# Two layer norms in each of two layers, rebuilt: squares relative to a mean of half the stream, the last two slabs tile by tile, no loop over layers

## The reference

```
for l in range(2):
    proj = x @ w_in                        # pool, q, k, v, conv and gate columns
    merged = sum of three gated branches   # pooling, windowed attention, short convolution
    x = layer_norm(ALPHA * x + merged @ w_o, ln1_g, ln1_b)
    up = causal_dwconv(x @ w_up, ffn_conv_w)      # 3 taps, D_FF_2 = 2816
    a, b = split(up, 2)
    x = layer_norm(ALPHA * x + (silu(a) * b) @ w_down, ln2_g, ln2_b)

def layer_norm(x, g, b):
    mu  = mean(x);  var = mean(square(x - mu))
    return (x - mu) * rsqrt(var + 1e-5) * g + b
```

## Time and profile before

| what | us |
| --- | --- |
| median of 3 runs | 3015.32 (3015.03 to 3015.91) |
| profiled execution | 3016.21 |
| its span, first to last instruction | 3014.4 |
| PE busy | 2943.7 (98%) |
| ACT busy | 1600.8 (53%) |
| DVE busy | 1022.2 (34%) |
| POOL busy | 411.4 (14%) |

### The profile page before, as it was taken

How to read it: one execution, slowest core, us unless ns; L and a number is a source line. 1 busy time by engine, 2 the same in 40 slices (tenths; PEclk the granted TensorE clock), 3 DMA queues, 4 the chain that set the end, 5 groups by cost and what they waited for, 6 DMA issues and landing times.

```text
span 3014.4 us, 36389 instructions
## 1 busy us (share of the span) xinstructions
PE 2943.7 (98%) x13318; PEld 2389.8 (79%) x13318; DVE 1022.2 (34%) x2094; ACT 1600.8 (53%) x2309; POOL 411.4 (14%) x477
## 2 busy tenths in 40 slices
PE   8999999999999999999998999999999899999997
PEld 6889888888886678888887887888877788788885
DVE  4533535321214754112135114323242511432324
ACT  6655656544445755444556445545454644454544
POOL 1111111111111001111110111111111011111111
PEclk9999999999999999999999999999999999999999
DMA  8666767788886319888882896787867398688785
GB/s 236 148 150 134 163 134 154 152 196 192 192 194 149 84 41 203 193 195 192 193 194 64 198 194 136 190 199 179 201 151 173 78 193 192 135 196 183 194 195 140
DMA packets 138147, 503.52 MB, mean 167 GB/s; under 512 B 15472, under 2 KB 15728, under 8 KB 137872
## 3 DMA queue, kind: packets, MB, share of 16 engines
q0 software_dynamic: 68016, 248.22, 46.6%
q1 hardware_dynamic: 69120, 251.69, 27.2%
q10 hardware_dynamic: 864, 1.65, 0.2%
HBM read 499.40 MB, written 2.10 MB: 166 GB/s over the span
## 4 chain that ended last, share of the span: by engine, by line
PE 87%; DVE 4%; DMA 3%; ACT 3%; issue 2%; DVEq 1%; ACTq 0%
PE ps L937 72%; PE ps L955 5%; DMA wl<-weights 3%; PE ps L1040 1%; PE ps L979 1%; PE ps L1097 1%; PE ps L1260 1%; ACT wl L418 1%; PE ps L1242 1%; PE ps L1241 1%; DVE arena L1906 1%; DVEq L1910 1%; DVE arena L1972 1%; PE ps L1314 0%; PE ps L1080 0%
## 5 line engine op out<-in xcount | busy, mean ns | idle before, releaser
L417 ACT ACTIVATE wh<-raw 128x1024 fp32r<-128x1024 f32 (+1 forms) x470 | 495.1, 1053 | 1103.4 <-PE ps L937 1055.6
L937 PE MATMUL ps<-HH,wh 128*128 128x512 f32 x2368 | 933.0, 394 | 13.2 <-DVE HL L1888 7.7
L937 PE MATMUL ps<-HH,wl 128*128 128x512 f32 x2368 | 924.3, 390 | 0.0
L937 PE MATMUL ps<-HL,wh 128*128 128x512 f32 x2368 | 924.3, 390 | 0.0
L399 POOL DMA_DIRECT2D wl<-weights x470 | 409.5, 871 | 2574.3 <-ACT wl L418 2574.1
L937 PEld LDWEIGHTS ps<-HH,wh 128*128 128x128 f32 x2368 | 446.2, 188 | 116.0 <-DVE HL L1888 10.1
L937 PEld LDWEIGHTS ps<-HL,wh 128*128 128x128 f32 x2368 | 446.1, 188 | 94.4 <-issue 3.1
L937 PEld LDWEIGHTS ps<-HH,wl 128*128 128x128 f32 x2368 | 446.2, 188 | 93.2
L418 ACT ACTIVATE wl<-raw 128x1024 fp32r<-128x1024 f32 (+1 forms) x470 | 488.2, 1039 | 0.0
L937 PE MATMUL ps<-MH,wh 128*128 128x512 f32 x1120 | 437.2, 390 | 1.6 <-DMA wl<-weights 0.7
L937 PE MATMUL ps<-MH,wl 128*128 128x512 f32 x1120 | 435.8, 389 | 0.0
(11 more groups left out here) (254 smaller groups left out, 2535.7 us busy)
## 6 DMA issues: line engine op xcount, KB each, us to landing
raw<-weights SPq DMA_DIRECT2D x472, 512.0 KB, 6.7
wl<-weights POOLq DMA_DIRECT2D x470, 512.0 KB, 7.9
XT<-x SPq DMA_DIRECT2D x4, 512.0 KB, 6.0
out<-XT SPq DMA_DIRECT2D x4, 512.0 KB, 2.7
arena<-tables POOLq DMA_DIRECT2D x1, 1024.0 KB, 11.4
arena<-table_h ACTq DMA_DIRECT2D x1, 640.0 KB, 5.7
arena<-swaps_a POOLq DMA_DIRECT2D x1, 576.0 KB, 8.2
lpar<-layers ACTq DMA_DIRECT2D x2, 218.0 KB, 2.9
```

Of the source, the lines that this page charges most:

```text
L417: act_f(wh[:, n, 0:w], raw[:, n, 0:w], ACT.Copy)
L937: op = mm(bank(g, t), w[:, slot, at:at + P], x[:, first + kt, :], start=(kt == 0 and w is wh and x is xh), stop=(kt == n_k - 1 and w is wl))
```

## The change

closing() takes the place of the last residual set and the norm behind it, on all three engines.

- When the first half of the stream (tiles 0 to 3) has its residual, DVE adds its four tiles and PE makes their mean with a matrix of 2/D (ln_half, ln_mean), after the first slab of the last set. DVE subtracts this mean from all eight tiles before the last set has ended; ACT squares tiles 0 to 3 then.
- The last two slabs of the set run tile by tile, so that output tiles 0 to 2 end earlier (ln_tile). DVE adds each to the stream, and sums of tiles and squares are carried along on DVE.
- After the last product PE makes the mean of what is left (ln_off) and the mean of the squares (ln_ms). The variance is the mean of squares less the squared mean (dsq, rsH), and DVE subtracts the second mean tile by tile, ahead of the scaling.
- Scaling is in place in XT, without the buffer of three. HH comes from XT, HL follows, and the stream's own beta (and ALPHA) is added at the end for all eight tiles.
- ACT's slab copies are placed by hand inside the norm, one of them split in its two copies. The table of Ln and Exp is loaded earlier: before the last set of the gates' w_o and in the last up part.
- PE has four dummy sums instead of two, and none in norm 4.
- The last norm makes no HH and HL. ACT adds beta in XT and raises x_final for the output.
- The layers and the parts of the MLP are written out (turns, H_PARTS) instead of looped; the parts are 3, 4 and 4 sets. PE's loop over the gates stays.

The core of the diff:

```diff
-H_PART = dict(slab=24, group=6, split=8, up=4)
-H_LAYER = dict(slab=120, group=56, split=4 + 8 + 8 + 2 * UP_SETS + 8, att=16, hl=1, sq=16, pre=2, ln=2, ts=2, up=UP_SETS)
+H_PARTS = ((0, 3), (3, 4), (7, 4))
+H_LAYER = dict(slab=120, group=54, split=4 + 8 + 8 + 2 * UP_SETS + 8, att=16, hl=1, sq=16, ln=2, ts=2, up=UP_SETS)
...
+def turns(c, runs, adds):
+    for i in range(runs):
+        with c.stage(**adds):
+            yield i
...
-                sp.wait_ge(split_done, TOTAL_SPLITS - KT + 2 * n + 2)
+                sp.wait_ge(x_final, 2 * DEPTH2 * KT - KT + 2 * n + 2)
...
+            def closing(nslab, beta, end=False):
+                g, s, gl = c.take("group"), c.take("slab", nslab) + SLOTS, c.take("group")
+                n, ln = c.take("sq", KT), c.take("ln")
+                x0 = ln.times(4)
+                c.take("ts")
+                high_parts(s, 1)
+                for t in range(KT):
+                    if t == 4:
+                        high_parts(s + 1, nslab - 3)
+                    if t == 7:
+                        high_part(s + (nslab - 2))
+                    if t < 4:
+                        act.wait_ge(ln_x, x0.value(t + 1))
+                    else:
+                        wait_taken(act, g, t - 3)
+                    act_f(sq8[t], XT[:, t, :], ACT.Square).then_inc(sq_ready, 1)
+                act.wait_ge(ln_off, ln.value(1))
+                act_f(dsq, bank(gl, 1), ACT.Square).then_inc(ln_dsq, 1)
+                less_high_part(s + (nslab - 2))
+                act.wait_ge(ln_var, ln.value(1))
+                act_f(rsH, rsH, ACT.Ln, bias=cst[:, C_EPS5:C_EPS5 + 1])
                 act.drain()
                 act_f(rsH, rsH, ACT.Exp, scale=-0.5).then_inc(ts_ready, 1)
-                c.take("ts")
-                s = c.take("split", KT)
+                p = c.take("split", KT)
                 for t in range(KT):
-                    act.wait_ge(split_src, (s + t).value(1))
-                    act_f(HH[:, t, :], hfH[:, t % NHF, :], ACT.Identity,
-                          bias=lpar[:, beta + t:beta + t + 1]).then_inc(split_hi, 1)
-
-            def up_part(sets, first):
+                    act.wait_ge(split_src, (p + t).value(1))
+                    bias = lpar[:, beta + t:beta + t + 1]
+                    if end:
+                        act_f(XT[:, t, :], XT[:, t, :], ACT.Identity, bias=bias).then_inc(x_final, 1)
+                        continue
+                    act_f(HH[:, t, :], XT[:, t, :], ACT.Identity, bias=bias).then_inc(split_hi, 1)
+                    if t == 1:
+                        high_part(s + (nslab - 1))
+                    if t == 2:
+                        less_high_part(s + (nslab - 1))
+                if end:
+                    high_parts(s + (nslab - 1), 1)
...
+                if first == H_PARTS[-1][0]:
+                    log_and_exp()
                 set_of(sets)
-                set_of(sets)
-
-            with c.loop(act, DEPTH2, H_LAYER) as layer:
+                if first != H_PARTS[-1][0]:
+                    set_of(sets)
+            for layer in turns(c, DEPTH2, H_LAYER):
...
+                log_and_exp()
                 set_of(4)
-                set_of(4)
-                layer_norm(L_LN1B)
-                with c.loop(act, 2, H_PART) as part:
-                    up_part(4, part * 16)
-                up_part(UP_SETS - 8, 32)
-                layer_norm(L_LN2B)
+                closing(4, L_LN1B)
+                for first, sets in H_PARTS:
+                    up_part(first, sets)
...
+            def closing(nslab, xh, xl, end=False):
+                g, s, gl = c.take("group"), c.take("slab", nslab), c.take("group")
+                ln, n = c.take("ln"), c.take("sq", KT)
                 c.take("ts")
+                n_k = 2 * nslab
+                def products(j, t):
+                    slot = (s + j).mod(SLOTS)
+                    for k in range(2):
+                        kt, at = 2 * j + k, k * 512 + t * P
+                        for w, x in ((wh, xh), (wh, xl), (wl, xh)):
+                            op = mm(bank(g, t), w[:, slot, at:at + P], x[:, kt, :],
+                                    start=(kt == 0 and w is wh and x is xh), stop=(kt == n_k - 1 and w is wl))
+                    return op
                 wait_set_free(pe, g)
-                pe.wait_ge(pre_ready, c.take("pre").value(1))
-                mm(bank(g, 0), mean_w, t1H, start=True, stop=False)
-                for t in range(4, KT):
-                    wait_taken(pe, g + (-1), t % 4 + 1)
-                    op = mm(bank(g, 0), mean_w, XT[:, t, :], start=False, stop=(t == KT - 1))
-                op.then_inc(ln_mean, 1)
-                g = c.take("group")
-                wait_set_free(pe, g)
-                sum_squares(g, mean_w, sqH)
+                for j in range(nslab - 2):
+                    wait_low(s + j)
+                    for t in range(4):
+                        op = products(j, t)
+                    op.then_inc(w_used, 1)
+                    if j == 0:
+                        wait_set_free(pe, gl)
+                        pe.wait_ge(ln_half, ln.value(1))
+                        mm(bank(gl, 0), half_w, t1H, start=True, stop=True).then_inc(ln_mean, 1)
+                for t in range(4):
+                    for j in (nslab - 2, nslab - 1):
+                        if t == 0:
+                            wait_low(s + j)
+                        op = products(j, t)
+                        if t == 3:
+                            op.then_inc(w_used, 1)
+                    if t < 3:
+                        op.then_inc(ln_tile, 1)
+                pe.wait_ge(ln_rest, ln.times(2).value(1))
+                mm(bank(gl, 1), mean_w, t1H, start=True, stop=False)
+                wait_taken(pe, g)
+                mm(bank(gl, 1), mean_w, XT[:, KT - 1, :], start=False, stop=True).then_inc(ln_off, 1)
+                pe.wait_ge(ln_rest, ln.times(2).value(2))
+                mm(bank(gl, 2), mean_w, sq8[0], start=True, stop=False)
+                pe.wait_ge(sq_ready, n.value(KT))
+                mm(bank(gl, 2), mean_w, sq8[KT - 1], start=False, stop=True).then_inc(ln_ms, 1)
+                if not end:
+                    keep_clock(gl, 4)
                 return c.take("split", KT)
...
+            def closing(nslab, scale, gamma, beta, end=False):
+                g, s, gl = c.take("group"), c.take("slab", nslab), c.take("group")
+                ln, ts, n = c.take("ln"), c.take("ts"), c.take("sq", KT)
+                x = [XT[:, t, :] for t in range(KT)]
+                def add(dst, a, b):
+                    return v.tensor_tensor(dst, a, b, ALU.add)
+                dve.drain()
+                add(t1H, x[0], x[1])
+                add(t2H, x[2], x[3])
+                dve.drain()
+                add(t1H, t1H, t2H).then_inc(ln_half, 1)
                 dve.wait_ge(ln_mean, ln.value(1))
+                for t in range(4):
+                    v.tensor_tensor(x[t], x[t], bank(gl, 0), ALU.subtract).then_inc(ln_x, 1)
+                for t in range(4, KT):
+                    if scale is None:
+                        v.tensor_tensor(x[t], x[t], bank(gl, 0), ALU.subtract)
+                    else:
+                        v.scalar_tensor_tensor(out=x[t], in0=x[t], scalar=scale, in1=bank(gl, 0),
+                                               op0=ALU.mult, op1=ALU.subtract)
+                dve.wait_ge(sq_ready, n.value(4))
+                add(sq8[0], sq8[0], sq8[1])
+                add(sq8[2], sq8[2], sq8[3])
+                dve.drain()
+                add(sq8[0], sq8[0], sq8[2])
+                dve.drain()
+                for t in range(4, KT):
+                    if t < KT - 1:
+                        dve.wait_ge(ln_tile, ln.times(3).value(t - 3))
+                    else:
+                        wait_used(dve, s + (nslab - 1))
+                    add(x[t], bank(g, t - 4), x[t]).then_inc(acc_free[g.mod(2)], 1)
+                    if t == KT - 1:
+                        break
+                    if t > 4:
+                        dve.drain()
+                        op = add(t1H, x[4], x[5]) if t == 5 else add(t1H, t1H, x[t])
+                        if t == KT - 2:
+                            op.then_inc(ln_rest, 1)
+                    dve.wait_ge(sq_ready, (n + t).value(1))
+                    op = add(sq8[0], sq8[0], sq8[t])
+                    if t == KT - 2:
+                        op.then_inc(ln_rest, 1)
+                    dve.drain()
+                def off(t):
+                    return v.tensor_tensor(x[t], x[t], bank(gl, 1), ALU.subtract)
+                def scaled(t):
+                    v.scalar_tensor_tensor(out=x[t], in0=x[t], scalar=lpar[:, gamma + t:gamma + t + 1],
+                                           in1=rsH, op0=ALU.mult, op1=ALU.mult).then_inc(split_src, 1)
+                p = c.take("split", KT)
+                def low(t):
```

(29 more changed lines are left out.)

135 lines of the change are left out of this document (43 added, 92 removed).

## The result

The changed kernel took 2987.64 us (median of 4 runs, 2984.13 to 2989.49), the kernel before 3015.18 beside it (4 runs, 3011.88 to 3015.91): ratio 0.9909, 95% interval 0.9892 to 0.9927. A second measurement on another chip gave 0.9898 (0.9882 to 0.9915). The profiled execution took 2989.49 with a span of 2987.5, against 3016.21 and 3014.4. Forecast for it: 2981.6. The change is faster, as forecast, but by 0.9% instead of 1.1%: 6.6 to 7.9 us of the forecast gain are missing.

What follows compares the result with a forecast made beforehand. PE's products were taken as the bound (72% of the chain). Gains of 17.1 + 5.8 + 12.0 (norms) - 2.6 (table loads) + 1.5 (up sets) + 0.8 (attention) = 34.6 us gave 2981 us, range 2974 to 2991.

Steps and rivals of the forecast that it cites:

- forecast case: Whole kernel: the summed terms hold without any rival, some 2981 us within 2976 to 2986; chance 0.68.
- The norm from E: From PE's last product issued before a norm to the first after it: 8.9 us instead of 17.56.
- Half mean +0.86 a norm: Early mean of four tiles: hidden under products, but its matmul stands among them, costing 0.86 us a norm.
- first rival: Weights come late in the closings, 1 to 2 us in four norms: 2987 us; chance 0.12.
- Fifth slab: Weights after a norm: PE waits 1.0 us behind norms 1 and 3; some 6 behind norm 2, reached at E+36.7.
- Clock behind the norms: PE's clock drop after norms 1 to 3, costing 1.7 us of PE time at norm 1, was taken as gone.
- norm 4, priced at 12.0: Last norm, last product to the end: 19.1 us instead of 31.97, a gain of 12.0 after 0.86 for the extra matmul.
- third rival: The end waits for the last, unused slab, landing at E+27.7 against E+19.1: 2990 us; chance 0.05.
- Table load, -1.3 a layer: Ln and Exp table load ahead of the last down projection: 1.28 us in a tight chain, 2.6 lost over two layers.
- Attention, +0.8: Attention part: fewer register waits in written-out code gain 0.8 us, bounds 0 to +3.
- Up sets, +1.5: MLP up sets: shorter ACT and DVE handshakes in written-out code gain 1.5 us, bounds 0 and +7.
- Instruction starvation: Rival for the written-out layers: engines starve for instructions, slower than before, 3062 us at 1.5 us a block; chance 0.02.

Runs made afterwards that it cites:

- experiment 11: Changed kernel with PE's half-mean sum moved from behind the first slab to behind the closing's last product; 3045.21 us, ratio 1.011.
- experiment 7: Changed kernel with the last two slabs run slab by slab again instead of tile by tile; 2997.64 us, ratio 0.9952.
- Experiment 10: Beyond experiment 4, ACT makes the fifth slab's two copies between its HH tiles 4, 5 and 6 of norms 1 to 3; 2969.48 us, ratio 0.9859.
- experiment 6: Changed kernel without the four dummy sums of each norm that keep PE's clock; 2985.23 us, ratio 0.9915.
- experiment 9: Changed kernel measured again without any edit, on a third chip; 2982.24 us, ratio 0.9898.
- Experiment 2: Changed kernel, but ACT copies two slabs before it waits for h_ready and loads the layer's numbers; 2979.66 us, ratio 0.9894.
- experiment 1: Changed kernel without the last norm's copy and transfer of the very last, unused slab; 2977.79 us, ratio 0.9887.
- experiment 3: Changed kernel with the Ln and Exp table loaded two slab copies later in the last up part; 2983.59 us, ratio 0.9908.
- Experiment 5: Kernel before with only its loops over layers and MLP parts written out; 3007.23 us against 3011.63, ratio 0.9987.
- experiment 4: Changed kernel without the unused slab, with layer numbers and table loaded later, and low(0) ahead of scaled(1); 2973.43 us, ratio 0.9877.
- experiment 8: Changed kernel whose last norm makes HH and HL and adds beta behind all tiles, like the others; 2986.97 us, ratio 0.9925.

## Why the prediction was right, and where it was not

The direction, the size of the norms' gain and nearly every moment inside them came as argued. The total is less well met: 2987.64 lies above the 2976 to 2986 of the forecast case alone, and inside the stated 2974 to 2991 only by what the rivals added to it. The rival that came true was the one with a chance of 0.05, and that it cost 4.8 us and not the 8.6 of its own price kept the time within the range; that part is luck.

- **The norm from E, priced at 8.9.** Right: 9.35, 9.0, 9.0. Its two halves were tested: without the early half mean it is 25.3 at norm 2 (experiment 11), without the order by tiles 11.1, and 13.3 from the last product (experiment 7).
- **Half mean +0.86 a norm, otherwise hidden; first rival (weights late in the closings).** Right; no closing waits inside. The stretch from the first gate product (1635.64) to E of norm 1 is 219.4 us, before 218.2: 0.86 and 0.35 more.
- **Fifth slab.** Forecast waits of 1.0 behind norms 1 and 3 and some 6 behind norm 2; the rows have 1.27, 1.17 and 5.22 between products, a product's own 0.23 included. Experiment 10 showed what set them: ACT's order. That norm 2's 36.7 came so near (35.84) is in part luck, since the traces with the same code have 33.9 to 36.1.
- **Clock behind the norms.** Gone, as forecast; experiment 6 showed that the four sums of keep_clock do it, and that the time does not show what they are worth while the fifth slab is late.
- **What failed first: the clock behind norm 2's wait.** The prediction argued from one row, a stand of 2.18 us with full clock behind it, and then forecast a stand of 6 us without asking the same question of it. It cost 2.7 us in the first profile and 1.1 in experiment 9's. Experiment 2 cut the wait to 1.42 us, and no drop followed.
- **What failed most: norm 4, priced at 12.0, measured 7.2** (31.97 less 23.89, less the half mean's 0.86). The steps up to the output were right to a tenth (experiment 1). The third rival was the true one, with a wrong reason against it: "no instruction waits for it". No instruction of the kernel does; POOL's drain at the end of the program does, and it ends 0.2 us after the slab has landed. Its moments were right (POOL at E+18.3, forecast 18.4), its size was not: the 9.3 us from issue to use were read where the DMA engines were busy (0.98 in the earlier trace rows); at the end this transfer is nearly alone (0.52 of 0.61 MB) and lands after 5.1 us. The drain stands in the trace of before as well, from 2985.1 to 2990.7, where it lay under work. I had put 0.05 on it.
- **Table load, -1.3 a layer.** 1.88 and 1.85 from product to product, 1.6 of each a wait; the load itself 1.28, as its row said. Over the sixteen closings counted under experiment 3 the wait comes in ten, so the term fits this profile better than the kernel's average.
- **Attention, +0.8.** Wrong in sign but small. In layer 2 it took 45.31 us to the first product against 45.0; in layer 1 the first gate product came 0.84 later. In the kernels of experiments 1 to 10 other than 5, whose code there is the changed kernel's, layer 1's stretch takes 44.9 to 46.3 us and layer 2's 44.6 to 45.3, so this term could not be told from nothing.
- **Up sets, +1.5.** Too low: with the known additions taken off (0.86, and 1.6 of wait ahead of the closing), the two long stretches won 1.8 and 2.4 us. Experiment 5 won 3.3 and 1.7 in them by writing out alone. Single traces do not fix such a term: the kernel before ranged over 8.6 us within one measurement.
- **Instruction starvation.** No sign of it: the longest stretch without a product outside norms and attention is the fifth slab's.

## What to carry to other kernels

Of a tail behind the last product, ask first which of its operations need the last tile at all; here one sum put early enough hid the vector work of seven of eight tiles, and the same sum put late made the kernel slower than before. Then follow every in-order queue past the new end, through the last instructions of the program: work for nobody (a prefetch beyond the last tile) is free only while something else ends later. And where a trimmed latency comes back as a wait for weights, look at what the copying engine does before it issues them; two copies put into gaps of that queue brought the fifth slab 1.8 to 1.9 us earlier at each of three norms, with no operation saved (0.9877 to 0.9859; the intervals of the two times overlap, the traces do not).

## What the runs showed of the hardware that I had not expected

- **The clock's answer to a stand.** Between two products at the fifth slab behind norm 2, ten traces give this series. Gaps of 1.42, 1.78 and 2.19 us (experiments 2, 6, 4): full clock behind. Gaps of 3.30 (8), 3.30 (11), 3.55 (3), 3.87 (1), 4.22 (7), 5.22 (changed kernel) and 5.46 (9): none, 2.1, 5.1, 3.4, 4.7, 5.1 and 2.1 us of products at double distance. So in this place no gap up to 2.2 us was followed by half clock and six of seven from 3.3 us on were, but the length of the low stretch does not follow the length of the gap. And in experiment 5 the same two stands in the same code were followed by it once in three times, in experiment 7 a stand of 1.8 us before f32 sums three times in four. A term for the clock is therefore a range: here 0 to 2.7 us.
- **f32 sums at half clock.** Two f32 matmuls of 128x512 take up to 2.08 us instead of 1.02 behind a stand of 1.8 us (experiment 7, at norms 2 to 4) or 12.8 us (experiment 11).
- **POOL's last drain.** It starts with POOL's last transfer and ends 0.2 to 0.35 us after that transfer has landed, in all thirteen traces; it took 5.4 to 5.9 us. In the changed kernel, where the transfer was issued 0.5 us before SP was through, it ended the kernel; in experiments 1, 4, 8 and 10 and in the kernels with the old norms the transfer had landed long before, and the end followed the output.
